# Feed-forwards' way in with seven products in place of eight

## The reference

```
def swiglu(h, w_in, w_out):
    gate, up = jnp.split(h @ w_in, 2, axis=-1)
    return (jax.nn.silu(gate) * up) @ w_out

x = x + mx[5] * swiglu(modulate(rms_norm(x, norm2_g[i]), mx[3], mx[4]), ffn_w_in[i], ffn_w_out[i])
```

## Time and profile before

| | |
|---|---|
| median of 3 runs | 3027.04 us (3026.23 to 3032.28) |
| span of the profiled execution | 3029.1 us |
| TensorE busy | 2864.1 us, 95% |
| VectorE, ScalarE, POOL busy | 1450.7, 1221.4, 1332.4 us |
| mean granted TensorE clock | 0.976 of full speed |

### The profile page before, as it was taken

How to read it: one execution, slowest core, us unless ns; L and a number is a source line. 1 busy time by engine, 2 the same in 40 slices (tenths; PEclk the granted TensorE clock), 3 DMA queues, 4 the chain that set the end, 5 groups by cost and what they waited for, 6 DMA issues and landing times.

```text
span 3029.1 us, 41310 instructions
## 1 busy us (share of the span) xinstructions
PE 2864.1 (95%) x15994; PEld 2151.8 (71%) x15994; DVE 1450.7 (48%) x2336; ACT 1221.4 (40%) x1993; POOL 1332.4 (44%) x770
## 2 busy tenths in 40 slices
PE   7999989999999899999999999998888989989997
PEld 4878768888888789898878888783663348556533
DVE  3556656532321734334441112656565656557665
ACT  5666542111112533333342222436335653454464
POOL 3665425444533435444355555477440027763100
PEclk9999999999999999999999999999999979999999
DMA  6102314433321112112133332220358843124694
GB/s 248 43 22 83 141 74 155 149 144 134 126 76 62 57 49 77 63 56 76 44 122 98 98 97 91 70 84 21 113 209 334 343 144 98 42 65 187 268 398 188
DMA packets 85968, 374.88 MB, mean 124 GB/s; under 512 B 9424, under 2 KB 11984, under 8 KB 76688
## 3 DMA queue, kind: packets, MB, share of 16 engines
q1 hardware_dynamic: 68640, 311.75, 28.9%
q10 hardware_dynamic: 12528, 43.73, 3.7%
q0 software_dynamic: 4608, 16.78, 1.5%
HBM read 556.77 MB, written 29.36 MB: 194 GB/s over the span
## 4 chain that ended last, share of the span: by engine, by line
PE 81%; DVE 7%; DMA 3%; POOL 3%; ACT 3%; issue 2%; SPq 0%; DVEq 0%; POOLq 0%; ACTq 0%
PE PS L106 79%; PE PS L109 2%; DMA ALL<-in_moe 2%; DVE SCR L121 1%; DMA BF<-in_ada 1%; POOL RTX L121 1%; DVE XF L127 1%; DVE SM L121 1%; ACT SCR L115 1%; DVE RTX L118 1%; POOL XF L124 1%; ACT RT L115 1%; POOL RT L121 1%; POOL WL L121 0%; DVE SCR L127 0%
## 5 line engine op out<-in xcount | busy, mean ns | idle before, releaser
L106 PE MATMUL PS<-RT,WH 128*128 128x512 f32 (+1 forms) x5632 | 1508.6, 368 | 40.6 <-DVE RT L127 9.1
L106 PEld LDWEIGHTS PS<-RT,WH 128*128 128x128 f32 x5632 | 1010.9, 190 | 263.0 <-issue 30.8
L121 POOL TENSOR_TENSOR WL<-RAW,WH 128x1024 fp32r<-128x1024 f32 x284 | 704.9, 2484 | 716.9 <-ACT WH L115 716.9
L106 PE MATMUL PS<-RT,WL 128*128 128x512 f32 (+1 forms) x2816 | 927.2, 365 | 0.0
L115 ACT ACTIVATE WH<-RAW 128x1024 fp32r<-128x1024 f32 x284 | 299.0, 1056 | 592.1 <-PE PS L106 531.9
L106 PEld LDWEIGHTS PS<-RT,WL 128*128 128x128 f32 x2816 | 491.4, 190 | 59.6
L121 POOL TENSOR_TENSOR RT<-SCR,RT 128x512 fp32r<-128x512 f32 (+2 forms) x146 | 197.9, 1364 | 324.5 <-ACT RT L115 231.9
L106 PE MATMUL PS<-RTX,SCR 128*32 128x512 f32 x1176 | 286.3, 621 | 7.3 <-DMA RTX<-placed_out,PLACE 7.3
L106 PE MATMUL PS<-ALL,SCR 128*32 x576 | 268.8, 611 | 24.0 <-DVE SCR L121 14.3
L121 DVE TENSOR_TENSOR SCR<-PS,SCR 128x512 f32<-128x512 f32 (+1 forms) x106 | 58.9, 572 | 469.8 <-PE PS L106 455.2
L127 DVE SCALAR_TENSOR_TENSOR XF<-PS,SM,XF 128x512 f32<-128x512 f32 x240 | 151.1, 658 | 244.3 <-PE PS L106 244.0
(11 more groups left out here) (272 smaller groups left out, 3750.1 us busy)
## 6 DMA issues: line engine op xcount, KB each, us to landing
ALL<-in_moe SPq DMA_DIRECT2D x100, 2048.0 KB, 7.7
ALL<-in_moe SPq DMA_DIRECT2D x100, 1024.0 KB, 14.2
RAW<-in_ff SPq DMA_DIRECT2D x132, 512.0 KB, 3.6
BF<-in_ada SPq DMA_DIRECT2D x64, 512.0 KB, 4.7
RAW<-in_ret SPq DMA_DIRECT2D x64, 512.0 KB, 3.3
RTX<-in_ada SPq DMA_DIRECT2D x30, 512.0 KB, 7.0
RAW<-in_win SPq DMA_DIRECT2D x28, 512.0 KB, 3.4
XF<-placed_in ACTq DMA_DIRECT2D x24, 512.0 KB, 8.7
```

The source lines that it names most:

```text
L106: return NOTHING if self.e is None else self.e.matmul(o, w, x, start=first, stop=last)
L121: return NOTHING if self.e is None else self.e.tensor_tensor(*a)
```

## The change

For each hidden tile but the first, gate and up are the rows, two halves of the features the inner index and two halves of the tokens the columns of a 2 x 2 by 2 x 2 block product. The eight block products become seven (`GROUP`), with sums of weight quarters (four per tile, `piece_add`, VectorE) and sums of activation quarters (`SUMS`, T1 to T4, once per feed-forward, VectorE). A pass has half the tokens as columns: 384 in `ff0`, 256 in `ff1`. Four PSUM banks per tile hold results; three are copied out by ScalarE (`COPY`) before TensorE accumulates further into them, and VectorE (U2, u1, G2) and POOL (s75, u2) add up gate and up of each token half.

Weights of the way in and out go through the slots as pieces of 128 x 512, six in place of three units. The remainder of a piece is made by POOL, but for product 0 of a tile in `ff0` and products 0, 4 and 6 in `ff1`, which VectorE makes (`low_engine`). SP loads units in halves (`load_half`). In the normalization ScalarE now biases every feature tile twice (rounded, and in place), and feature tiles go in the order `K_ORDER`. The chunks are 4, 4, 4, 4, 4 and 2. The reductions of `dve_ada1` are spread one or two to a hidden tile and one to an output tile, with four load buffers for six. A constant of the retention stage is loaded at the end of `ff0`, and the small hidden layer of the second block moves one chunk earlier in `ff1`.

The core of the diff:

```diff
-CHUNKS = (4, 4, 4, 4, 3, 3)
+CHUNKS = (4, 4, 4, 4, 4, 2)
...
+GROUP = (("a", "B11", True), ("q", "T3", True), ("p", "T1", True), ("r", "T2", True), ("q", "T4", False),
+         ("p", "B22", False), ("a", "B21", False))
+K_ORDER = (0, 4, 1, 5, 2, 6, 3, 7)
...
+        def low_engine(s, n):
+            kind, i, q = PIECES[n]
+            return dve_done if kind == "mix" and q in {"ff0": (0,), "ff1": (0, 4, 6)}[s] else pool_done
...
+        def piece_high(act, s, n):
+            hi, lo = piece(s, n)
+            wait_slot(act, s, n)
+            held = raw_of_piece(s, n)
+            if held:
+                wait_half(act, s, *held)
+                act.activation(hi, raw_half(s, *held), ACT.Copy).then_inc(*act_done.done(("phi", s, n)))
+            else:
+                act.wait_ge(*dve_done.at(("sum", s, n)))
+                act.activation(hi, piece_sum(s, n), ACT.Copy).then_inc(*act_done.done(("phi", s, n)))
...
+        def sum_over(n):
+            kind, i, q = PIECES[n]
+            return n + {2: 1, 3: 2}[q] if kind == "mix" and q in (2, 3) else None
+        def piece_low(eng, done, s, n):
+            hi, lo = piece(s, n)
+            held = raw_of_piece(s, n)
+            eng.wait_ge(*act_done.at(("phi", s, n)))
+            if sum_over(n):
+                eng.wait_ge(*dve_done.at(("sum", s, sum_over(n))))
+            x = raw_half(s, *held) if held else piece_sum(s, n)
+            events = [("plo", s, n)]
+            if PIECES[n][0] == "half" and PIECES[n][2] == 1:
+                events.append(("lo", W.first[s] + PIECES[n][1]))
+            eng.tensor_tensor(lo, x, hi.bitcast(F32), ALU.subtract).then_inc(*done.done(*events))
...
+            if q == 1:
+                wait_half(dve, s, i, 0)
+                wait_half(dve, s, i + 1, 0)
+                dve.tensor_tensor(o, raw_half(s, i, 0), raw_half(s, i + 1, 0), ALU.subtract).then_inc(*dve_done.done(("sum", s, n)))
...
+        def sum_upto(dve, s, event):
+            while W.next_sum < len(W.items):
+                u, stage, n = W.items[W.next_sum]
+                if stage is not None:
+                    if u > W.first[s] or W.piece_left_at(stage, n) > pe_done.value(event):
+                        return
+                    if PIECES[n][0] == "mix" and PIECES[n][2] in (1, 2, 3, 5):
+                        piece_add(dve, stage, n)
+                    if low_engine(stage, n) is dve_done:
+                        piece_low(dve, dve_done, stage, n)
+                W.next_sum += 1
...
-            while W.next_low < len(UNITS):
-                u = W.next_low
+            while W.next_low < len(W.items):
+                u, s, n = W.items[W.next_low]
+                if s is not None:
+                    if u > last or W.piece_left_at(s, sum_over(n) or n) > pe_done.value(event):
+                        return
+                    W.next_low += 1
+                    if low_engine(s, n) is pool_done:
+                        piece_low(pool, pool_done, s, n)
+                    continue
...
+        SUMS = (("T1", ("B12", "B11")), ("T3", ("B22", "B12")), ("T2", ("B22", "T1")), ("T4", ("B21", "T2")))
+        T_ORDER = ("T3", "T1", "T2", "T4")
+        T_LOW = {"T3": "dve", "T4": "dve", "T1": "pool", "T2": "pool"}
...
+            for k in K_ORDER:
+                for j, _, n in parts:
+                    act.wait_ge(*dve_done.at(("h", s, k, j)))
+                    act.activation(operand_halves(s, k, 0, j, operand), normed(s, k)[:, :, part_of_half(j)], ACT.Identity,
+                                   bias=B[:, 8 * j + k:8 * j + k + 1]).then_inc(*act_done.done(("hi", s, k, j)))
+                for j, _, n in parts:
+                    h = normed(s, k)[:, :, part_of_half(j)]
+                    act.wait_ge(*act_done.at(("hi", s, k, j)))
+                    act.activation(h, h, ACT.Identity, bias=B[:, 8 * j + k:8 * j + k + 1]).then_inc(*act_done.done(("hb", s, k)))
+            for kk in range(4):
+                for x in T_ORDER:
+                    act.wait_ge(*dve_done.at((x, s, kk)))
+                    act.activation(operand(s, x, kk, 0), plain_operand(s, x, kk, 1), ACT.Copy).then_inc(*act_done.done((x, s, kk)))
...
+                if k >= 4:
+                    ff_norm_low(dve, dve_done, s, k - 4, parts)
+            for kk in range(4):
+                dve.wait_ge(*act_done.at(("hb", s, kk + 4)))
+                for x, (a, b) in SUMS:
+                    if x in ("T2", "T4"):
+                        dve.wait_ge(*dve_done.at((b, s, kk)))
+                    dve.tensor_tensor(plain_operand(s, x, kk, 1), normed_half(s, a, kk), normed_half(s, b, kk), ALU.subtract
+                                      ).then_inc(*dve_done.done((x, s, kk)))
+            for x in ("T3", "T4"):
+                for kk in range(4):
+                    t_low(dve, dve_done, s, x, kk)
+        def ff_norm_pool(pool, s, parts, before):
+            free_h(pool, before)
+            for kk in range(4):
+                ff_norm_low(pool, pool_done, s, kk + 4, parts)
+            for x in ("T1", "T2"):
+                for kk in range(4):
+                    t_low(pool, pool_done, s, x, kk)
...
+        def pe_ff_group(pe, s, c, f):
+            fi = hidden_tile(c, f)
+            for q, (name, x, opens) in enumerate(GROUP):
+                n = mix_at(c, f, q)
+                wait_piece(pe, s, n)
+                if opens:
+                    o = take_bank(pe, (s, name, fi), HALF[s])
+                else:
+                    o = bank.of((s, name, fi))[:, 0:HALF[s]]
+                    pe.wait_ge(*act_done.at((s, "copy", name, fi)))
+                for kk in range(4):
+                    if fi == 1 and x[0] == "T":
+                        pe.wait_ge(*act_done.at((x, s, kk)))
+                        pe.wait_ge(*(dve_done if T_LOW[x] == "dve" else pool_done).at(("tlo", x, s, kk)))
+                    w = [y[:, P * kk:P * kk + P] for y in piece(s, n)]
+                    events = [("pc", s, n)] if kk == 3 else ()
+                    if opens:
+                        three(pe, o, w, operand_pair(s, x, kk), kk == 0, kk == 3, events)
+                    else:
+                        three_onto(pe, o, w, operand_pair(s, x, kk), events)
...
+            blocks = [(m, k) for k, m in itertools.product(range(nf), range(2))]
+            blocks += [(m, k) for m, k in itertools.product(range(2, 8), range(nf))]
+            for b, (m, k) in enumerate(blocks):
+                n = out_at(c, 0, 0) + b // 4
+                if b % 4 == 0:
+                    wait_piece(pe, s, n)
...
+                    if m == 0:
+                        pe.wait_ge(*pool_done.at((s, "act", c, k, j)))
...
+                    sum_upto(dve, s, ("pc", s, mix_at(c, f, 2)))
+                    dve.wait_ge(*pe_done.at(("pc", s, mix_at(c, f, 3))))
+                    dve.wait_ge(*act_done.at((s, "copy", "a", fi)))
+                    u2 = COPY["a"][:, 0:nh]
+                    dve.tensor_tensor(u2, bank.of((s, "r", fi))[:, 0:nh], u2, ALU.add).then_inc(*dve_done.done((s, "U2", fi)))
+                    bank.give((s, "r", fi), dve_done.now())
+                    sum_upto(dve, s, ("pc", s, mix_at(c, f, 3)))
+                    dve.wait_ge(*dve_done.now())
+                    dve.wait_ge(*pe_done.at(("pc", s, mix_at(c, f, 4))))
+                    dve.tensor_tensor(UP[:, 0:nh], bank.of((s, "q", fi))[:, 0:nh], u2, ALU.add).then_inc(
+                        *dve_done.done((s, "u1", fi)))
+                    bank.give((s, "q", fi), dve_done.now())
+                    sum_upto(dve, s, ("pc", s, mix_at(c, f, 4)))
+                    dve.wait_ge(*pe_done.at(("pc", s, mix_at(c, f, 5))))
+                    if fi >= 2:
+                        dve.wait_ge(*pool_done.at((s, "act", fi - 2)))
+                    dve.tensor_tensor(v2, bank.of((s, "p", fi))[:, 0:nh], u2, ALU.add).then_inc(*dve_done.done((s, "G2", fi)))
+                    bank.give((s, "p", fi), dve_done.now())
+                    sum_upto(dve, s, ("pc", s, mix_at(c, f, 5)))
+                    sum_upto(dve, s, ("pc", s, mix_at(c, f, 6)))
+                    dve.wait_ge(*pool_done.at((s, "u2", fi)))
+                    dve.wait_ge(*act_done.at((s, "silu", fi, 1)))
+                    dve.tensor_tensor(v2, v2, COPY["q"][:, 0:nh], ALU.mult).then_inc(*dve_done.done())
+                    dve.wait_ge(*act_done.at((s, "silu", fi, 0)))
+                    dve.wait_ge(*dve_done.at((s, "u1", fi)))
+                    dve.tensor_tensor(v1, v1, UP[:, 0:nh], ALU.mult).then_inc(*dve_done.done((s, "act", fi)))
...
+                    lo_upto(pool, ("pc", s, mix_at(c, f, 0)))
+                    if f:
+                        pool_tile_low(pool, s, c, f - 1, parts)
+                    lo_upto(pool, ("pc", s, mix_at(c, f, 1)))
+                    s7, s5, u2 = (COPY[x][:, 0:nh] for x in ("q", "p", "a"))
+                    pool.wait_ge(*act_done.at((s, "copy", "p", fi)))
```

(53 more changed lines are left out.)

458 lines of the change are left out of this document (379 added, 79 removed).

## The result

The changed kernel takes 3099.1 us (median of 4 runs, 3090.0 to 3109.7) against 3029.7 for the kernel before on the same chip: 1.023 times as long, 95% interval 1.0205 to 1.0253. Slower was forecast, by 38 us, to 3066; it is 69. The profiled execution has a span of 3107.9 us against 3029.1.

What follows compares the result with a forecast made beforehand. TensorE, busy nearly throughout both feed-forwards, was taken to bound the kernel. Losses of 101 us (starts, chunks, ends, clock) less a gain of 62.6 made it 38 us slower, 3066 us; own range 3040 to 3095, wider 3000 to 3100.

Steps and rivals of the forecast that it cites:

- Gain: TensorE passes in both feed-forwards: fewer or narrower passes save 62.6 us.
- the pass prices: TensorE time from pass start to pass start: 0.1745 us for 384 columns, 0.1198 for 256.
- Starts: Second tile of each feed-forward: token sums and remainders taking turns start it 19.2 and 12.7 us later.
- Chunks: Tiles and chunk ends: VectorE and POOL late for TensorE, costing 28, 9.5, 12, 8 and 8 us.
- POOL's written order: Chunk ends: six way-out remainders, 7.4 us, stand ahead of the last tile's activation remainder that TensorE wants.
- the exclusion: VectorE operations between SBUF tiles and POOL operations hold each other off, so their times add: 12.1 us against TensorE's 10.06.
- the raw halves: Raw weights loaded in halves, asked for about four pieces (6 us or more) before use: costed at nothing.
- one of the signs named: In the windows, VectorE's sums of 0.69 us would be drawn out to 1.9 us.
- After the two long waits I put 1.7 us each, 3.4: Behind the two start waits, TensorE's granted clock falls for a while: 1.7 us each, 3.4 in all.
- the clock falls at every chunk end as well: Rival: some 12 stretches of lower clock at 1.7 us more, 3087 us and up; chance 0.12.
- the slots hide the lateness: Rival: late pieces are made up inside the six weight slots, 57.5 us of chunk lateness goes, 3008 us; chance 0.22.
- the operations don't exclude each other: Rival: no exclusion between these VectorE and POOL operations, starts at 18, ends at 8, 2990 us; chance 0.09.

Runs made afterwards that it cites:

- the filled kernel: The changed kernel with 11 to 31 extra passes of 512 columns, sums thrown away, at the head of each chunk's way out: 3081.5 us (1.0169).
- the shortened reductions: The changed kernel with the first feed-forward's 64 VectorE reductions taken over 8 columns instead of 1024: 3075.5 us (1.015).
- the last two runs: Changed kernel, seven products in first feed-forward only, chunk-end orders mended, start reordered by need: 3003.5 us; with remainders also moved from POOL to VectorE: 2999.4 us.

## Why the prediction was right in sign and short in size

**Gain.** 62.6 forecast, 63.8 measured: the pass prices held (0.1738 for 0.1745, 0.1199 for 0.1198).

**Starts.** 19.2 and 12.7 forecast as later starts; the second tile starts at 472.3 instead of 475.5 (15.9 us later than before), with a first tile that ended 2 us earlier than forecast. Waits of 13.9 and 9.4: somewhat too high, by taking every turn between VectorE and POOL as lost. Of VectorE's four sums for a pair of feature tiles three took 0.55 us and one 1.35.

**Chunks.** 24 us forecast for the first feed-forward (12, 8 and half of the last chunks' 8), 21.0 measured; 41.5 for the second, 42.2 measured. The size is right and its cause half so, which makes the agreement in part luck. POOL's written order and the exclusion are in it (both shown above), but so are the raw halves, which I costed at nothing because each is asked for four pieces ahead. At a chunk's end they are not in time: SP's request waits for the remainder that frees the buffer, and ScalarE's queue waits for the landing with SiLU behind it. The sentence in the prediction that names this price, "each late half would hold ScalarE, and behind it every later piece", is what happened. And one of the signs named came out weaker: VectorE's weight sums, to be drawn out to 1.9 us, took 0.99 to 1.05 on average (first feed-forward, 500 to 950 us).

**The term that failed** is "After the two long waits I put 1.7 us each, 3.4". It leaves the time 4 us above the forecast's own range (3040 to 3095) and 1 us inside the wider one (3000 to 3100). Slow passes cost 37 us more than before, of which the filled kernel puts 21 down to the clock behind the chunk ends' idle stretches; some 8 lie about the two starts, and 8 are handoffs too short to count as waits, which I had not priced either. That is my rival "the clock falls at every chunk end as well", to which I gave 0.12: it came on top of the forecast's own losses. Its evidence, one low stretch behind an idle 3.58 us, applied to every chunk end at which I forecast a wait of 3 us or more; a forecast of those waits should have carried the clock with it.

**Rivals.** That the slots hide the lateness was wrong by 63 us of waits (by the prediction's own terms, 62.6 - 43, lateness of some 20 us and not 24 makes up the gain); that the operations don't exclude each other is refuted by the shortened reductions.

## What to carry to other kernels

A wait of TensorE has a price beyond itself: here the chunk ends' waits of 2.7 to 7.2 us cost some four tenths more in slow passes behind them (21 us for 49.9). Whoever forecasts the one should forecast the other. Where a remainder is late, follow it back through every engine's written order and down to the transfer that frees the buffer: two orders held it here; mending one took off 37 us, mending the other alone added 18, and both took off 50. A form that saves passes is worth using only where the engines that feed it have room: here in the first feed-forward (25 us faster than before), not in the second.

## What the runs showed of the hardware

VectorE and POOL do not always take turns. In the last two runs VectorE went on without a break and one POOL subtraction stayed out all the while: 9.55 us where the three behind it took 0.96 each, and 8.48 where one of its shape takes 1.30. It went in when VectorE paused (at 472.1 in the one, for 0.1 us at 467.1 in the other). But VectorE's readiness alone does not decide it. In the change's own trace both engines run without a break from 463.7 to 470.2 us and take strict turns: VectorE's starts lie 1.27 us apart from 464.16 on, POOL's as well from 465.06 on.

```profile
463.69 4.36 DVE L148 TENSOR_TENSOR RT<-RTX,RT 128x384 fp32r<-128x384 f32 x4
465.06 5.10 POOL L148 TENSOR_TENSOR BFR<-BF,BFR 128x384 fp32r<-128x384 f32 x4
```

What decides between the two was not tried.

Idle stretches of one length were not always followed by the lower clock. In the change's first feed-forward, four chunk ends have a wait of 2.66 to 2.71 us; behind three of them the granted clock fell, behind the one at 725.4 it did not. Two of the four, in the 3 us behind the wait (2.70 and 2.66 us):

```profile
820.43:823.40 2.97, 2.97 (x9) 2.49 (x10) 0.89 (x2) 0.00 (x0) 1.08 (x1) 0.50 0.21 68
725.39:728.40 3.01, 3.00 (x17) 2.65 (x18) 1.80 (x3) 0.63 (x1) 1.10 (x1) 1.00 0.22 63
```

What made the difference the runs do not show.
